# A decoder step on one core: a third key buffer, key products first, convolution sums in PSUM, another order for the heads, and x turned tile by tile

## The reference, cut to what matters

```python
h = rmsnorm(x);  z = h @ w_in                    # 1024 -> 5760 columns
A: u = a * sigmoid(b); c = causal depthwise conv, width 31, 384 channels; layernorm; silu; @ w_conv_out
B: dilated attention, 12 heads of 32 in 3 groups (window, dilation) = (128,1), (512,4), (2048,16); @ w_dil_out
C: block-sparse attention, 4 heads of 64: of the full past blocks of 256 keys the top 3 by q . mean_k(block),
   and the own block, are attended; @ w_moba_out
x += (sum_b sigmoid(gate_b) * branch_b) @ w_out
x += relu(rmsnorm(x) @ w_ff1)^2 @ w_ff2          # 1024 -> 4096 -> 1024
```

## Time and profile before

| what | value |
|---|---|
| median of 3 runs | 536.91 us |
| the three runs | 535.6, 536.91, 538.85 us |
| the profiled execution, its own time | 536.93 us |
| its span | 535.0 us |
| mean granted TensorE clock, as a share of full | 0.944 |
| busy: PE, DVE, ACT, POOL | 483.2, 341.2, 231.9, 158.9 us |

### The profile page before, as it was taken

The page is one execution under the profiler, slowest core; times in us unless marked ns, Lnnn a source line. Parts: engine busy times, 40 slices in busy tenths (PEclk is TensorE's granted clock), DMA queues, the critical chain, the costliest instruction groups (busy, mean ns, idle before and its releaser), DMA issues.

```text
span 535.0 us, 9294 instructions
## 1 busy us (share of the span) xinstructions
PE 483.2 (90%) x3673; PEld 443.1 (83%) x3673; DVE 341.2 (64%) x471; ACT 231.9 (43%) x425; POOL 158.9 (30%) x90
## 2 busy tenths in 40 slices
PE   3999778799858979979976999999999999999997
PEld 1988577799748869958754889899999999999997
DVE  3136547589999784798541687787777774434440
ACT  6553245245236434405165526555445443333430
POOL 2871543887457625702210507100000000000000
PEclk9998799899788979979897899999999999999999
DMA  9983849699865847717887528269899989698900
GB/s 276 365 331 115 317 153 373 230 384 397 284 242 184 274 158 263 247 41 288 318 322 267 183 59 256 62 183 342 255 336 332 251 298 289 222 263 304 291 10 20
DMA packets 86235, 130.91 MB, mean 245 GB/s; under 512 B 2806, under 2 KB 82076, under 8 KB 83620
## 3 DMA queue, kind: packets, MB, share of 16 engines
q1 hardware_dynamic: 82669, 93.99, 54.8%
q0 software_dynamic: 2992, 35.98, 17.6%
q10 hardware_dynamic: 543, 0.51, 0.3%
HBM read 128.09 MB, written 24.74 MB: 286 GB/s over the span
## 4 chain that ended last, share of the span: by engine, by line
PE 71%; DVE 18%; ACT 4%; issue 3%; POOL 3%; DMA 1%; SPq 0%; ACTq 0%; DVEq 0%
PE ps L1015 35%; PE ps L684 7%; PE ps L685 6%; PE ps L686 6%; DVE ca L1454 5%; DVE sm L1427 5%; DVE kv L1423 2%; PE ps L832 2%; PE ps L924 2%; PE ps L893 2%; POOL rawlo L615 2%; PE ps L919 1%; PE ps L651 1%; ACT logits L1217 1%; DVE q L1414 1%
## 5 line engine op out<-in xcount | busy, mean ns | idle before, releaser
L684 PE MATMUL ps<-acts,whi 128*128 128x264 f32 x424 | 132.1, 311 | 19.5 <-POOL rawlo L615 11.9
L615 POOL TENSOR_TENSOR rawlo<-raw,whi 128x1024 fp32r<-128x1024 f32 x48 | 119.5, 2505 | 72.5 <-ACT whi L1103 72.3
L685 PE MATMUL ps<-acts,whi 128*128 128x264 f32 x424 | 127.0, 299 | 0.0
L686 PE MATMUL ps<-acts,rawlo 128*128 128x264 f32 x384 | 115.2, 300 | 0.0
L684 PEld LDWEIGHTS ps<-acts,whi 128*128 128x128 f32 x424 | 86.9, 205 | 27.1 <-POOL rawlo L615 13.8
L1730 DVE TENSOR_TENSOR ws<-fraw,ws 128x1024 fp32r<-128x1024 f32 x64 | 78.2, 1221 | 40.2 <-ACT ws L1309 40.1
L1015 PE MATMUL ps<-as,ws 128*128 128x264 f32 x768 | 94.7, 284 | 0.0
L1015 PEld LDWEIGHTS ps<-as,ws 128*128 128x128 f32 x768 | 93.3, 188 | 0.2
L1015 PE MATMUL ps<-hs,ws 128*128 128x264 f32 x768 | 93.1, 283 | 0.0
L1015 PEld LDWEIGHTS ps<-hs,ws 128*128 128x128 f32 x768 | 92.9, 188 | 0.1
L685 PEld LDWEIGHTS ps<-acts,whi 128*128 128x128 f32 x424 | 87.1, 205 | 0.0
(11 more groups left out here) (241 smaller groups left out, 541.0 us busy)
## 6 DMA issues: line engine op xcount, KB each, us to landing
fraw<-in_w_ff SPq DMA_DIRECT2D x32, 1024.0 KB, 8.1
raw<-in_w_in SPq DMA_DIRECT2D x14, 1536.0 KB, 10.3
out_dk_s<-in_state_dil_k SPq DMA_DIRECT2D x8, 1023.5 KB
out_dv_s<-in_state_dil_v SPq DMA_DIRECT2D x8, 1023.5 KB
ebias<-bias_rows SPq DMA_DIRECT2D x4, 512.0 KB, 7.4
out_dk_s<-in_state_dil_k SPq DMA_DIRECT2D x8, 255.5 KB
out_dv_s<-in_state_dil_v SPq DMA_DIRECT2D x8, 255.5 KB
raw<-in_w_in SPq DMA_DIRECT2D x3, 512.0 KB, 8.5
```

The lines of the kernel that those rows point to most:

```text
L615: pool.tensor_tensor(raw_unit(u, True), raw_unit(u), whi[u % WR][:, :, :].bitcast(F32), ALU.subtract).then_inc(wlo_ready, 1)
L684: pe.matmul(out, hi, acts[0][:, k], start=k == 0, stop=False)
L685: pe.matmul(out, hi, acts[1][:, k], start=False, stop=False)
L686: return pe.matmul(out, lo, acts[0][:, k], start=False, stop=k == KD - 1)
```

## The change

It has these parts.

1. A third key buffer kv[2] is laid over `gates` (from gate unit 8 on) and the early tiles that lie there (`xnat`, `hot`). The items' buffers are given by `SLOT`. The load of s = 3..7 waits for `sum_heads(s-3)`; that of s = 2 waits for the tables and x to be read. `take` of gate unit 8 waits for `kred_done` 6.
2. The queries go from PSUM straight into q2; `qnat` is gone. The spread queries are two to a bank, and four of them follow unit 5.
3. On DVE all eight key products and head sums come first, with no taps or prompt heads between; `new_products` goes to POOL.
4. The taps accumulate in PSUM banks 2 and 3 (`taps_at`); only the last tap writes `ca`. Channel tile 2 has a chain of its own, the other two are interleaved. The taps are spread over the gaps of the samples' chain.
5. The prompt heads move: scores after units 32, 36 and 41, in banks 4 to 6. `CHAIN` is 32, with one free unit after `route`. The values start with `values_moba(0)` after unit 41.
6. `turn_h` turns tile by tile over all eight banks as each tile is scaled, behind 12 idle products (`warm`); `high(0)` comes before the groups are taken out.
7. Two rounds of `copy_state`, and the copies of the first group, move from the chunks 6, 8 and 9 to the feed-forward loads.

```diff
+SLOT = [0, 1, 2, 0, 1, 2, 0, 1] + [0] + [1, 0] * 4
-        SPREAD_BANK = [4, 5, 4, 5, 4, 7, 7, 7] + [6, 7] * 4
+        SPREAD_BANK = [4, 4, 5, 5] * 2 + [6, 7, 3, 4, 5, 6, 7, 3]
+        SPREAD_WAITS = [0] * 4 + [2, 2, 4, 4] + [0, 0, 0, 8, 8, 9, 10, 11]
-        SPREAD_AT = {5: (0, 1), 8: (2,), 12: (3,), 16: (4,), 21: (5,), 27: (6,), 31: (7,), 33: (8, 9),
-                     34: (10, 11, 12, 13, 14, 15)}
-        SCORES_AT, TURN_AT, VALUES_AT = [26, 32, 41], [31, 35], [32, 36]
-        CHAIN = 34
-        KV_AT = [8, 11, 15, 20, 24, 30, 33, 36, 39, 44, 44, 44, 44, 44, 44]
+        SPREAD_AT = {5: (0, 1, 2, 3), 13: (4, 5), 19: (6, 7), 27: (8, 9, 10), 30: (11, 12), 31: (13, 14, 15)}
+        SCORES_AT = {32: 0, 36: 1, 41: 2}
+        EXP_AT = {34: 0, 38: 1, 42: 2}
+        SCALE_AT = {35: 0, 39: 1, 43: 2}
+        TURN_AT = {36: 0, 40: 1, 44: 2}
+        VALUES_AT = {38: 0, 42: 1, 44: 2}
+        CHAIN = 32
+        SUMS = ["m0", "m1", "d"] + [f"m{n}" for n in range(2, NS)]
+        SUMS_AT = {41: (0,), 42: (1,), 43: (2,), 44: (3,)}
+        KV_AT = {1: 0, 3: 1, 10: 2, 12: 3, 15: 4, 18: 5, 20: 6, 23: 7, 28: 8, 31: 9, 34: 10}
...
-                if c in (6, 8):
-                    copy_state(c // 2 - 3)
...
+                if s == 2:
...
+                    copy_state(0)
+            copy_state(1)
             with sp.Fori(1, 4) as i:
...
-                if 2 <= s <= IT_V + 1:
+                if s == 2:
+                    pool.wait_ge(bias_made, 2)
+                    pool.wait_ge(rows_out, 16)
+                    pool.wait_ge(x_turned, KD)
+                elif 3 <= s <= 7:
+                    pool.wait_ge(kred_done, s - 2)
+                elif 8 <= s <= IT_V + 1:
                     pool.wait_ge(kred_done, s - 1)
...
+            def warm():
+                pe.wait_ge(first_in, 16)
+                for _ in range(WARM):
+                    pe.matmul(ps[:, KD - 1, 0:P], ident, ident, start=True, stop=True)
             def turn_h():
...
+                for k, (t, n) in enumerate(((2, NS), (0, P), (1, P))):
+                    pe.wait_ge(x_scaled, k + 1)
+                    for i in range(KD):
+                        ins = pe.transpose(ps[:, i, t * P:t * P + n], xs[0:n, t, i * P:(i + 1) * P], ident[0:n, 0:n])
+                        if t == 1:
+                            ins.then_inc(h_turned, 1)
...
+            high(0)
             for i in range(KD):
                 sc.wait_ge(h_turned, i + 1)
...
-                if i == 2:
-                    high(0)
+                if i == 5:
+                    high(1)
...
+        def taps_at(c):
+            return ps[:, 3, 0:SEQ] if c == 2 else ps[:, 2, c * SEQ:(c + 1) * SEQ]
...
-            def taps(lo, hi):
+            def taps(cs, lo, hi):
...
-                    for c in range(KC):
-                        src, acc = uext[:, c, k:k + SEQ], ca[:, c, 0:SEQ]
+                    for c in cs:
+                        src, acc = uext[:, c, k:k + SEQ], taps_at(c)
...
-                            v.wait_ge(conv_step, KC * (k - 1) + c + 1)
-                            v.scalar_tensor_tensor(acc, src, w[:, c, k:k + 1], acc, ALU.mult, ALU.add
-                                                   ).then_inc(conv_step, 1)
+                            v.wait_ge(conv_step[c], k)
+                            v.scalar_tensor_tensor(ca[:, c, 0:SEQ] if k == TAPS - 1 else acc, src, w[:, c, k:k + 1], acc,
+                                                   ALU.mult, ALU.add).then_inc(conv_step[c], 1)
```

DVE's order from the fifth key product on, before and after:

```diff
             score_cache(5)
-            taps(0, 13)
-            prompt_logits(0)
             sum_heads(5)
-            new_products()
             score_cache(6)
-            prompt_probs(0)
             sum_heads(6)
             score_cache(7)
-            prompt_logits(1)
             sum_heads(7)
-            prompt_probs(1)
+            taps((0, 1), 0, 4)
             score_state()
+            prompt_logits(0)
             sample_logits()
+            taps((2,), 0, 6)
             select_blocks()
+            taps((2,), 6, 11)
             selection_row()
+            prompt_probs(0)
+            taps((2,), 11, 16)
             sample_maxima()
+            taps((2,), 16, 26)
             spread_maxima()
+            taps((2,), 26, TAPS)
+            prompt_logits(1)
             subtract_maxima()
-            taps(13, 19)
+            taps((0, 1), 4, 8)
+            prompt_probs(1)
             sample_sums()
-            taps(19, 21)
-            sample_denominators()
+            taps((0, 1), 8, 14)
             prompt_logits(2)
-            taps(21, 27)
+            taps((0, 1), 14, 20)
             prompt_probs(2)
-            taps(27, TAPS)
+            taps((0, 1), 20, TAPS)
             sample_taps()
             prompt_logits(3)
             conv_center()
+            sample_denominators()
+            prompt_probs(3)
             outputs_dilated()
-            prompt_probs(3)
```

More of the change, by code:

```diff
@@ L281, in build_layer @@
         wo_in = [sem(f"wo_in{s}") for s in range(2)]
-        kv_in = [sem(f"kv_in{s}") for s in range(2)]
+        kv_in = [sem(f"kv_in{s}") for s in range(3)]
         e_in = [sem(f"e_in{s}") for s in range(2)]
@@ L539, in _ @@
                 load_ff(0, s, False)
+                if s == 2:
+                    for src, dst in ((state[0][0], state[0][2]), (state[0][1], state[0][3])):
+                        a = src.rearrange("l n w h e -> (l n) (w h e)")[:, P:P * P]
+                        b = dst.rearrange("l n w h e -> (l n) (w h e)")[:, 0:(P - 1) * P]
+                        sp.dma_start(b, a).then_inc(copied, 16)
+                    copy_state(0)
+            copy_state(1)
             with sp.Fori(1, 4) as i:
@@ L727, in natural @@
                     pe.wait_ge(x_copied, KD)
+                elif i > 3 and NAT[i - 2][0] == "q":
+                    pe.wait_ge(q_split, sum(x[0] == "q" for x in NAT[:i - 1]))
                 elif i > 3:
-                    pe.wait_ge(nat_evac, i - 1)
+                    pe.wait_ge(nat_evac, sum(x[0] != "q" for x in NAT[:i - 1]))
                 if kind in "qk":
@@ L835, in values_moba, with sums, turn_sums @@
                 ins.then_inc(pvm_done, 1)
-            def turn_moba(n):
-                pe.wait_ge(vo_ready, n + 2)
-                for t in range(2):
-                    ins = pe.matmul(ps[:, 7, t * 32 + 4 * n:t * 32 + 4 * n + 4], vo[:, t * P:(t + 1) * P], cst("pick4"),
-                                    start=True, stop=True)
+            def sums(i):
+                if i == 0:
+                    pe.wait_ge(exp_done, 3)
+                    pe.wait_ge(padded, 3)
+                else:
+                    pe.wait_ge(vo_ready, i)
+                if SUMS[i] == "d":
+                    values_dilated()
+                else:
+                    values_moba(int(SUMS[i][1:]))
+            def turn_sums(i):
+                pe.wait_ge(vo_ready, i + 1)
+                for half in range(2):
+                    if SUMS[i] == "d":
+                        at, width, pick = 64 + 16 * half, 16, "pick16"
+                    else:
+                        at, width, pick = half * 32 + 4 * int(SUMS[i][1:]), MH, "pick4"
+                    ins = pe.matmul(ps[:, 7, at:at + width], vo[:, half * P:(half + 1) * P], cst(pick), start=True, stop=True)
                 ins.then_inc(vt_done, 1)
@@ L1161, in natural_out @@
                 sc.wait_ge(nat_done, i + 1)
+                if i == 0:
+                    sc.wait_ge(q2_clear, 1)
+                    sc.wait_ge(const_in, 16)
+                    sc.copy(pickq[:, :], cst("pickq", 2 * DH)).then_inc(pick_ready, 1)
+                if kind == "q":
+                    sc.copy(q2[0:NS, col:col + P], ps[0:NS, bank, 256:384]).then_inc(q2_hi, 1)
+                    return
                 if kind in "kv":
@@ L1170, in natural_out @@
                 else:
-                    rows, off = (qnat, col) if kind == "q" else (snat, {"k": 0, "v": 640, "u": 1280}[kind] + col)
-                    sc.copy(rows[:, off:off + P], ps[0:NS, bank, 256:384]).then_inc(nat_evac, 1)
+                    off = {"k": 0, "v": 640, "u": 1280}[kind] + col
+                    sc.copy(snat[:, off:off + P], ps[0:NS, bank, 256:384]).then_inc(nat_evac, 1)
             def exps():
@@ L1178, in exps, with sums_out @@
                 sc.activation(ln[:, :], ln[:, :], ACT.Exp).then_inc(exp_done, 1)
-            def values_out(n):
-                if n == 0:
+            def sums_out(i):
+                n = sum(x != "d" for x in SUMS[:i + 1])
+                if SUMS[i] == "d":
                     sc.wait_ge(pvd_done, 1)
@@ L1185, in values_out @@
                     sc.wait_ge(pvm_done, n)
[L1186 to L1188 removed]
+                if i:
+                    sc.wait_ge(vt_done, i)
+                if i and SUMS[i - 1] == "d":
+                    sc.copy(vd_t[:, :], ps[:, 7, 64:96]).then_inc(vd_copied, 1)
                 sc.copy(vo[:, :], ps[:, 7, 256:512]).then_inc(vo_ready, 1)
```

(3 more changed lines are left out.)

315 lines of the change are left out of this document (139 added, 176 removed).

## The result

The changed kernel takes 504.2 us (median of 4 runs, 502.41 to 505.64), the kernel before 537.0 in the same comparison: ratio 0.9386, 95% interval 0.9338 to 0.9434. The forecast was 504.6. The profiled execution took 505.64 us with a span of 503.8. Beside later variants the changed kernel was run again: 0.9415 (0.9372 to 0.9457). Medians hold every run and ratios only those in the chip's faster state, so a difference of medians and one of ratios can be some us apart.

A forecast was written before the change was run, and what follows sets the result against it. PE bound from 343 us, nearly from 292.6; earlier it waited behind POOL's cache loads and DVE's head sums, and taps and POOL disturbed each other. Terms -2.5 + 0.8 - 58.4 + 26.4 - 2.6 + 4 = -32.3 from 536.9: 504.6; range 491 to 522.

The forecast's parts named there:

- the reserve: Cache loads and weight chunks from 58 to 112 us leave no room for a late one: 4 us added.
- Start: Start to the end of unit 2: POOL with three low parts becomes the limit, 27.2 to 24.7 us, gain 2.5.
- To the first key product: From the end of unit 2: three more spread products of unit 5 add 0.8 us; first key product at 45.5.
- The key stage: First key product to last key sum: DVE alone plus waits of about 4 and 1 us, 83.1 us, gain 58.4.
- To the end of unit 44: From the last key sum: the moved work returns, with slow units after waits; 88.0 us, a loss of 26.4.
- To the first branch product: From the end of unit 44: two buffers bind the loads for m5 and m7; 39.7 us, gain 2.6.
- The rest: First branch product to the end: 242.4 us as before; if longer, the moved copies are the cause.
- A tap in PSUM: DVE's taps summing in PSUM: 0.40 us in pairs, upper bound 0.65 each, which would add 13 us.
- rival 1: Taps get dearer, no overlap in PSUM: 518 us, to 529 if maxima and scores slip; chance 0.12.
- Rival 2: Transfers bind: cache and weight loads queue, or the copies fall on the feed-forward loads; 512 to 524 us, chance 0.13.
- Rival 3: Taps with sums in PSUM still wait for POOL's low parts, units 30 to 44: 36 us, 541 in all; chance 0.05.
- Rival 4: DVE's sums were not what held PE, so the stalls only move: about 535 us, chance 0.04.

The follow-up runs named there:

- later page 1: Changed kernel with only cache page 1 loaded later, after the low part of unit 8 instead of 3: 498.1 us, 0.9270 of the kernel before.
- 26 taps: Changed kernel with the first 13 taps of channel tiles 0 and 1 put ahead of the eighth key product: 514.4 us, 0.9600 of the kernel before.
- copies early: Changed kernel with the state copies back after weight chunks 6, 8 and 9: 516.5 us, 0.9630 of the kernel before.
- both pages later and the other order: Changed kernel, cache pages 0 and 1 loaded after units 4 and 8, page 2 in the buffer the first sum frees: 497.3 us, 0.9276 of before.
- pages 0 and 1 later: Changed kernel with the first two cache pages loaded after the low parts of units 4 and 8, not 1 and 3: 498.2 us, 0.9294 of before.

## Why the prediction was right, step by step

The sum held: forecast 504.6, and 505.64 for the profiled execution. It held with errors of both signs, in us, measured less forecast: -0.9, +5.9, +2.1, -5.6, +1.0, +2.6 by stage and -4 for the reserve, together +1.1. Some 11.6 us too little and 10.5 too much were counted, so a total within 1 us is luck; most steps of the mechanism are not.

*Start.* -3.4 for -2.5. The limit named, POOL with the first three low parts, holds for the start of unit 0, which waits 2.71 us for its low part, and without the idle products for unit 2 as well. With them PE waits for no low part between 13.3 and 23.8 us, so there its own pace at a lowered clock (0.93 in the mean of the stage) sets the end of unit 2, under a microsecond later than without.

*To the first key product.* This is the step that failed: "+0.8, first key product 45.5". It counted the work and no transfer. The faster start moved three issues forward, page 0 by 3.6 us, page 1 by 1.9 and the chunk of units 9 to 11 by 3.3 (27.18 to 23.88), all beside a chunk that ACT needs at 28. The prediction had 4 us for late loads, but looked for them from 58 to 112 us; there ACT waits for no chunk and no product for its page. Place wrong, size about right. The later page 1 shows the cause by taking it away. The last key sum, forecast at 128.6, ended at 135.7, and 5 us of that were there at the first product.

*The key stage.* -56.3 for -58.4. DVE's waits for PE were 5.07, 2.33 and 0.85, 8.3 us in all, where 5 were counted. Shown by experiment, in us of the whole time: the order is worth 10 for the 10.4 tried (26 taps), the third buffer 6, room for the transfers 11.5.

*To the end of unit 44.* +20.8 for +26.4. The term that was too high: three units (34, 37 and 41) were counted at 5.0 instead of 3.0 for a slow clock after waits. In the profile after, 34 and 41 take 3.0 and 3.1 us, and 37 takes 4.5, so 4.4 of these 6 us didn't come. Units 33 and 36 are slow too, 4.5 us each, but there the chain stands on DVE and ACT. PE waits 0.73 at `route`, 1.77 at `turn_selection`, 1.17 before the second head's scores, 1.69 at `turn_probs(1)` and not at all at `turn_probs(0)`, all far from the 5 us that the prediction named as its sign of being wrong. The rest of the 5.6 us is small differences.

*To the first branch product.* 40.7 for 39.7. The chain over two value buffers is there (PE waits 0.93 and 1.86 us for pages), but the sums in another order, meant to relieve it, left 2.3 us of that wait and brought nothing measurable.

*The rest.* 245.0 for 242.4 in one execution, 243.0 in the other. The copies are not the cause, as 243.1 without them shows. In the first, DVE's additions in the second of the eight column tiles met POOL's low parts of the output weights, and PE then waited 3.25 us for DVE, in the other execution 0.7 (changed kernel, DVE's timeline; the same kind takes 0.43 undisturbed):

```profile
267.14 1.34 DVE L1733 TENSOR_TENSOR mtmp<-mtmp 128x264 f32<-128x264 f32 x1
268.52 2.48 DVE L1734 TENSOR_TENSOR mtmp<-mtmp 128x264 f32<-128x264 f32 x1
270.93 2.58 DVE L1738 TENSOR_TENSOR acts<-mtmp,acts 128x264 fp32r<-128x264 f32 x1
```

*A tap in PSUM.* 0.40 in pairs and 0.51 to 0.52 alone, as taken; the bound of 0.65 and rival 1 are out. The rule on fixed costs with a PSUM source, weighed in the prediction, doesn't show: 0.40 in either place. *Rival 2* is one transfer away: copies early 11.5 us, page 1 about 6.5 to 8. *Rival 3*, a block in spite of PSUM, is out by the 2.44 us for six taps. Its price was put at 36 us; with the taps back in SBUF DVE spent 20 us more on them (60.2 against 40.2), since not every low part meets a tap. *Rival 4*, that DVE's sums were not what held PE, is refuted by the gain itself and by the 26 taps.

## What to carry to other kernels

If a long chain on one engine feeds the rest of the kernel, put its items first and let other work of that engine fill the gaps behind it: here the order was worth more than another buffer. When an edit makes a stage start sooner, list the transfers that start sooner with it, and which older one they lie beside; the gain at the start can be lost to a load that used to have the bandwidth alone. And give an accumulator that is updated beside a busy POOL a place that leaves at most one of DVE's inputs in SBUF.

## What was not expected of the hardware

The first tap, an instruction with one tensor input, is blocked by a low part when it writes SBUF (2.00 us for two) and not when it writes PSUM (0.98 for two, the low part beside it as before). The same form on 32x8 elements, in the changed kernel, with a low part from 159.92 to 162.29 on POOL:

```profile
159.97 2.34 DVE L1532 TENSOR_SCALAR selb<-const,topf 32x8 f32<-32x8 f32 x1
```

In the variant with both pages later and the other order it falls between two low parts, and takes 0.22:

```profile
155.01 0.22 DVE L1532 TENSOR_SCALAR selb<-const,topf 32x8 f32<-32x8 f32 x1
```

The rule of two SBUF inputs alone doesn't cover it. The sign stood in the earlier trace rows: the three first taps of 9.84 us have one tensor input too, and the prediction put them under that rule. By the Trainium skill ("SBUF — State Buffer", "Who interferes with whom") this kind of instruction can also enter a mode of its own, if its operands meet certain conditions, and that mode takes the port shared with GpSimd. In keeping with that, undisturbed it is faster from SBUF to SBUF, 0.41 us at 166.00 with the taps in SBUF, than into PSUM, 0.55 at 151.39 with pages 0 and 1 later; into PSUM it takes the same 0.55 with a low part beside it (156.06 in the changed kernel). The mode itself was not tested apart.

The other surprise is how dear a late chunk is at the start: 7.25 us of waiting on ACT became 8.5 us at the first key product (50.5 to 42.0 with the pages later), since PE also ran at 0.81 of its clock over the stretch instead of 1.00. And of those 8.5 us, 5 to 6.5 reached the end.
